# A layer stack on one core: when VectorE sums a conditioning tile, and when GpSimd issues five transfers

## The reference

```python
m = jnp.where(strict, jnp.einsum("bhnid,bhnjd->bhnij", k_beta, k) * decay, 0.0)
uw = lax.linalg.triangular_solve(m + eye, rhs, left_side=True, lower=True, unit_diagonal=True)
```

```python
mod = (c_act @ w_mod + b_mod)[:, None, :]       # w_mod is 1024 x 6144
sh1, sc1, g1, sh2, sc2, g2 = jnp.split(mod, 6, axis=-1)
```

## Time and profile before

| | us |
|---|---|
| median of three runs | 1040.17 |
| lowest and highest | 1037.32, 1042.5 |
| the profiled execution, its own time | 1038.82 |
| its span in the trace | 1037.0 |
| TensorE busy in the span | 998.6 |
| VectorE busy | 849.4 |
| ScalarE busy | 608.5 |
| GpSimd busy | 101.6 |

### The profile page before, as it was taken

How to read it: one execution, slowest core, us unless ns; L and a number is a source line. 1 busy time by engine, 2 the same in 40 slices (tenths; PEclk the granted TensorE clock), 3 DMA queues, 4 the chain that set the end, 5 groups by cost and what they waited for, 6 DMA issues and landing times.

```text
span 1037.0 us, 20795 instructions
## 1 busy us (share of the span) xinstructions
PE 998.6 (96%) x7662; PEld 926.8 (89%) x7662; DVE 849.4 (82%) x1566; ACT 608.5 (59%) x1056; POOL 101.6 (10%) x115
## 2 busy tenths in 40 slices
PE   6999999999999999998989999999998899999996
PEld 6999998999998889988989998888776799998884
DVE  5899978898889979888879899867788876668856
ACT  5687534766666464575756666456364565545443
POOL 1014421000000000001100001001200210000001
PEclk9999999999999999999999999999999999999998
DMA  9674313777776868837887657834422158766852
GB/s 290 171 217 147 103 63 91 233 212 217 217 216 216 288 174 250 281 102 246 233 258 216 191 177 248 288 93 134 147 62 82 41 154 245 191 193 216 277 149 116
DMA packets 216194, 193.09 MB, mean 186 GB/s; under 512 B 6032, under 2 KB 193568, under 8 KB 216000
## 3 DMA queue, kind: packets, MB, share of 16 engines
q1 hardware_dynamic: 206560, 158.09, 51.3%
q0 software_dynamic: 9136, 33.51, 9.8%
q10 hardware_dynamic: 432, 0.61, 0.2%
HBM read 191.14 MB, written 1.06 MB: 185 GB/s over the span
## 4 chain that ended last, share of the span: by engine, by line
PE 83%; DVE 9%; ACT 4%; DMA 2%; issue 1%; POOL 1%; POOLq 0%; DVEq 0%; ACTq 0%; SPq 0%
PE ps L607 22%; PE ps L608 22%; PE ps L609 22%; PE ps L1316 3%; PE ps L1317 3%; PE ps L1315 3%; DVE wL L2192 2%; DMA raw<-in_f_w_up 1%; PE ps L888 1%; PE ps L875 1%; PE ps L1145 1%; DVE cv L2214 1%; ACT wH L1362 1%; PE ps L830 1%; DMA modw<-in_w_mod_t 1%
## 5 line engine op out<-in xcount | busy, mean ns | idle before, releaser
L1362 ACT ACTIVATE wH<-raw 128x1024 fp32r<-128x1024 f32 x298 | 313.1, 1061 | 257.3 <-PE ps L609 189.2
L2192 DVE TENSOR_TENSOR wL<-raw,wH 128x1024 fp32r<-128x1024 f32 x298 | 357.7, 1225 | 67.7 <-ACT wH L1362 66.7
L607 PE MATMUL ps<-yH,wH 128*128 128x256 f32 x704 | 195.5, 278 | 3.0 <-DVE wL L2192 3.0
L608 PE MATMUL ps<-yL,wH 128*128 128x256 f32 x704 | 194.4, 276 | 0.0
L609 PE MATMUL ps<-yH,wL 128*128 128x256 f32 x704 | 194.4, 276 | 0.0
L607 PEld LDWEIGHTS ps<-yH,wH 128*128 128x128 f32 x704 | 132.2, 188 | 3.4 <-DVE wL L2192 3.2
L608 PEld LDWEIGHTS ps<-yL,wH 128*128 128x128 f32 x704 | 132.2, 188 | 0.1
L609 PEld LDWEIGHTS ps<-yH,wL 128*128 128x128 f32 x704 | 132.2, 188 | 0.0
L607 PE MATMUL ps<-wH,aH 128*128 128x512 f32 (+1 forms) x308 | 119.4, 388 | 0.7 <-DVE aL L2192 0.6
L608 PE MATMUL ps<-wL,aH 128*128 128x512 f32 (+1 forms) x308 | 119.0, 386 | 0.0
L609 PE MATMUL ps<-wH,aL 128*128 128x512 f32 (+1 forms) x308 | 119.0, 386 | 0.0
(11 more groups left out here) (430 smaller groups left out, 2148.8 us busy)
## 6 DMA issues: line engine op xcount, KB each, us to landing
raw<-in_f_w_up SPq DMA_DIRECT2D x88, 512.0 KB, 5.0
raw<-in_w_ff SPq DMA_DIRECT2D x64, 512.0 KB, 4.5
modw<-in_w_mod_t POOLq DMA_DIRECT2D x48, 512.0 KB, 5.5
raw<-in_f_w_down SPq DMA_DIRECT2D x44, 512.0 KB, 4.5
raw<-in_a_w_in SPq DMA_DIRECT2D x32, 512.0 KB, 4.8
raw<-in_w_in SPq DMA_DIRECT2D x22, 512.0 KB, 4.4
raw<-in_w_kv SPq DMA_DIRECT2D x16, 512.0 KB, 5.3
raw<-in_a_w_out SPq DMA_DIRECT2D x8, 512.0 KB, 3.4
```

The source lines that it names most:

```text
L607: mm(o, l[0], r[0], start=first, stop=False, skip_group_check=check)
L608: mm(o, l[0], r[1], start=False, stop=False, skip_group_check=check)
L1362: fn(slot(wH, c), raw[:, c % RAW], ACT.Copy).then_inc(hi_done, 1)
L2192: return tt(o, x, hi.bitcast(F32), ALU.subtract)
```

## The change

Three things change, and nothing of what is computed.

1. In `delta`, the conditioning sum between `P_` and `T_` is left out at the first level (`e` is 0) and stays at the other three. All later sums move up by one place. `down0` gets one place more, at its unit 8, so that from there on the count is the same as before. GpSimd's `mod_fetch` calls around the delta rule are given counts that fit.
2. In `up1`, GpSimd issues only tile 30 where it issued `tb`, `rows_c` and tiles 30, 31 and 32 in one go. `tb` waits for the second tile of `up1`, `rows_c` for the sixth, tile 31 for the ninth and tile 32 for the thirteenth.
3. Tiles 40, 41 and 42 of the ring, which were issued in one go at the start of `ff1`, wait for its blocks 3, 6 and 9.

```diff
-MODS_WITH = {"down0": (1, 3, 4, 5, 6, 7, 9, 10, 11, 12, 13, 15, 17), "down1": (0, 1, 3, 5, 7, 9, 11, 13, 15, 17), "ff2": range(2, 18, 2)}
+MODS_WITH = {"down0": (1, 3, 4, 5, 6, 7, 8, 9, 10, 11, 12, 13, 15, 17), "down1": (0, 1, 3, 5, 7, 9, 11, 13, 15, 17), "ff2": range(2, 18, 2)}
...
-            mod_fetch(4)
+            mod_fetch(2)
             pool.wait_ge(tok_act, 6)
             ptt(tok[:, 0, 8:16], tok[:, 0, 8:16], wide(ke[:, 0:8], HK), ALU.mult).then_inc(scan_pool, 1)
-            mod_fetch(9)
+            mod_fetch(8)
...
             pool.wait_ge(mod_used, mod_before(MOD_LATE))
+            mod_fetch(46, 31)
+            pool.wait_ge(prod_done, PRODS["down1"] + 2)
             pool.dma_start(tb[:], a["tables"]).then_inc(tables_in, 16)
+            pool.wait_ge(prod_done, PRODS["down1"] + 6)
             pool.dma_start(rows_c[:], a["rows_c"][:, 1024:1664].partition_broadcast(P).rearrange("p a n -> p (a n)")).then_inc(tables_in, 16)
-            mod_fetch(46, 33)
+            for m in (31, 32):
+                pool.wait_ge(prod_done, PRODS["down1"] + 4 * m - 115)
+                mod_fetch(46, m + 1)
...
             pool.wait_ge(m_o, RET_H)
+            for m in (40, 41, 42):
+                pool.wait_ge(relu_done, 3 * (m - 39))
+                mod_fetch(64, m + 1)
             mod_fetch(64, MOD_TILES)
...
-                    mod_sums(1)
+                    if e:
+                        mod_sums(1)
```

## The result

The changed kernel takes 1033.93 us in the median of six runs (1032.39 to 1035.72), the kernel before 1039.34 us on the same chip. The two medians differ by 5.4 us. The ratio on record is 0.9934, with a 95% interval of 0.9907 to 0.9961: worked out from it, the change is 6.9 us faster, 4 to 10, and the 5.4 us lie inside. The profiled execution took 1034.53 us, its span is 1032.7 us.

What follows compares the result with a forecast made beforehand. TensorE, busy for 998.6 of 1037.0 us, was taken to bound the kernel. 0.7 + 1.6 + 3.0 = 5.3 us off the profiled 1038.82 gave 1033.5; half of 1.35 added made 1034.2 us, range 1031.5 to 1038.0.

Steps and rivals of the forecast that it cites:

- Idle time at level 0: In the delta rule's doubling, TensorE's idle time put down to `T_` goes without the sum: 0.7 us gained.
- The slow clock: Transposes behind the gap in the doubling run at full clock once the gap goes: 1.6 us gained, bounds 0 and 1.8.
- the first rival: In the doubling, the clock falls anyway or only in some runs: 3.7 us gained, 1035.8 us; chance 0.20.
- The sum at level 1: In the doubling, the sum that stays ends before `T_` can start: cost 0, bounds 0 and 0.4 us.
- `down0` and the order of the sums: The added place in `down0`: cost 0, bound 0.2 us; sums moved up before it: cost 0, up to 0.5 us.
- `up1`, 3.0 us: Second up product: with five transfers apart, weights land within 9.7 us and TensorE's idle time goes: 3.0 us gained.
- `ff1`, nothing: In `ff1`, TensorE is busy for 20.00 of 20 us, so spreading the three tiles gains nothing.
- The sum.: Whole program: 0.7 + 1.6 + 3.0 = 5.3 us off the profiled execution's 1038.82, giving 1033.5 us.
- The half of 1.35 us: Whole program: the median lay 1.35 us above the profiled execution; half was added, giving 1034.2 us.
- The last rival: More is gained, since stalls of the burst's kind were larger in the runs behind the median: 1031 us; chance 0.05.

Runs made afterwards that it cites:

- third run: Only the edit in `ff1` (tiles 40, 41 and 42 wait for its blocks), against the kernel before: ratio 0.9988 (0.9968 to 1.0008).
- second part alone: Only the edit in `up1` (its five transfers issued apart), against the kernel before: ratio 0.995 (0.9933 to 0.9966), 5.2 us.
- first part: Only the sum left out at the first doubling level, `down0`'s added place and fitting counts, against the kernel before: ratio 0.998 (0.9961 to 0.9999), 2.1 us.

## Why the prediction was right, and where it was short

1034.2 us was forecast and 1033.93 us measured.

**Idle time at level 0, 0.7 us.** Right: the idle time is gone in every profile without the sum, and stays at 0.72 us when the sum is left out elsewhere. The prediction read the sum's 2.78 us as slowed by GpSimd; the run without GpSimd's work shows it, and that the gap goes with that work too.

**The slow clock, 1.6 us.** At this place the mechanism and the size were right; over the whole program the gain is smaller. In the profiles with the idle time (before, the second and third run, the sum left out at level 1) the clock from 120 to 140 us is 0.91, four times of four; in those without it 1.00, ten times of ten. The drop follows the gap, also where the gap is closed by GpSimd's work and not by the sum. What the prediction didn't see is the drop at 168 us: three of the ten have it, and lose 1.3 us. So the doubling gave 2.3 us in seven profiles and 1.0 us in three, 1.9 us on the mean; 2.1 us were measured. The rule that the prediction drew from the Trainium skill (TensorE: Matmul & The Clock Gate, Part 1), that the number of slow matmuls differs from run to run, decided nothing at the gap of 0.72 us. But the first rival, that a clock term holds only in some runs, is half true for the whole program.

**The sum at level 1, nothing.** Right, with the reason: GpSimd got faster by 0.96 us and was done at 132.9 us (133.0 forecast), and the sum ended at 134.0 us (134.3 forecast), 0.66 us early.

**`down0` and the order of the sums, nothing.** Right in the trace; no run took it apart from the doubling.

**`up1`, 3.0 us.** The mechanism was right, the term too small. The landings were forecast at up to 9.7 us and were 8.6; for the lone transfers behind them 6 to 7 us were forecast, and they were at most 5.8. But the part is worth 5.2 us (3.5 to 7). The term was read from one execution in which the idle time of 3.0 us left the clock alone. In profiles with the burst the idle time was 3.0, 2.2, 2.4, 2.8, 2.8 and 2.1 us, and after two of these six (the third run and the one with GpSimd's work cut) the clock fell, for 1.7 us of work. That gives 2.55 + 0.57, some 3.1 us in the mean, so the profiles explain less than the timed runs show.

The clocks of the timed runs show where a good part of the rest is. Over the experiments the kernel before was timed 73 times. In 15 of them the mean granted clock was 0.992 or less, 0.990 in the mean, and the time 1044.1 us; in the other 58 they were 0.9945 and 1039.7 us. A clock lower by 0.0046 over 1040 us is 4.8 us of full-speed work, and the difference is 4.4 us: the longest runs spend it at the half clock. In the mean of all runs that is 0.9 us. No profile caught such a run, so the place isn't shown. Three of the ten runs with the sum left out at level 1 are of this kind, and none of the twelve of the third part alone, of the eleven of the second part alone, or of the 64 without the gap in the doubling (22 of these had the burst at the start of `up1`). So the low clock was seen only where both the gap and that burst were, 18 times in 95. 3.1 and 0.9 us make 4.0, inside the interval of the second part. Not every long run is of this kind: the longest of the first part (1041.2 us) had a clock of 0.996, and the longest of the third (1044.0 us) 0.994. What these spend stays open.

**`ff1`, nothing.** Not contradicted.

**The sum.** 5.3 us were forecast against the profiled execution, 5.3 us off 1039.34 would be 1034.0. That the forecast met the measured median so well is in part luck. The term of `up1` was too small by some 2 us, and the doubling's a little too large. The half of 1.35 us that was added was a guess, and the before median was 0.8 us lower in six runs than in three. The changed kernel's medians are 1033.93, 1033.42 and 1033.14 us on the three occasions, but those of the kernel before beside it are 1039.34, 1039.86 and 1041.25: the same change is 5.4, 6.4 and 8.1 us. The last rival, larger stalls in the runs behind the median, had part of the truth.

## What to carry to other kernels

Read what a burst of transfers does to the others by their time to landing, and compare that with the reserve of the ring: here about 2.5 to 2.8 us more per 1000 KB, and idle time from 10.5 to 12 us on. Bringing the burst under that was enough here; spreading it further, or moving the next one, gave nothing that could be told. When an instruction of VectorE takes twice its usual time, look at GpSimd first, and move the one that has no deadline. And price a stall of TensorE by several executions, with the granted clock of each: its length and what the clock does behind it change from one to the next, and one profile can miss the costly kind.

## What the runs showed of the hardware

A gap of 0.72 us between groups of 64 small matmuls was followed by the half clock in four profiles of four, one of 1.34 us behind the scan's transposes in three of fourteen, and idle times of 2.1 to 3.0 us between large products (128 by 256) in two of six. So the length of a gap alone doesn't tell here whether the clock falls. What TensorE did around it is the likely reason, but no run varied that alone.

Working beside each other cost both engines: the sum grew from 1.23 to 2.78 us, and the multiplication that GpSimd began meanwhile, at 128.30 us, from 2.35 to 3.33 us. The multiplications of the values that were under way when the sum began took as long as without it, 3.75 us for two in the traces before and after.
